# Gates, branch projections and merge by channel, merged in place; output product finished for one half of the tokens before the other

## What is computed

```python
up = jnp.einsum('bsnc,ncd->bsnd', branches, w_branch[l])
g = jax.nn.sigmoid(gate.reshape(B, S, N_BRANCH, D) + b_gate[l].reshape(N_BRANCH, D))
mixed = jnp.sum(g * up, axis=2) @ w_out[l]
h = layer_norm(DEEPNORM_ALPHA * h + mixed, ln1_g[l], ln1_b[l])
moe = hier_moe(h, ...)          # 16 experts, top-1 group of 4, top-2 within it
h = layer_norm(DEEPNORM_ALPHA * h + moe, ln2_g[l], ln2_b[l])
```

## Time and profile before

| what | before |
|---|---|
| median of three runs | 497.06 us |
| the profiled execution's own time | 497.06 us |
| its span in the profile | 495.3 us |
| PE busy | 458.8 us (93%) |
| DVE busy | 252.9 us (51%) |
| ACT busy | 158.8 us (32%) |
| POOL busy | 81.6 us (16%) |
| read from HBM | 139.46 MB |

### The profile page before, as it was taken

The page is one execution under the profiler, slowest core; times in us unless marked ns, Lnnn a source line. Parts: engine busy times, 40 slices in busy tenths (PEclk is TensorE's granted clock), DMA queues, the critical chain, the costliest instruction groups (busy, mean ns, idle before and its releaser), DMA issues.

```text
span 495.3 us, 6108 instructions
## 1 busy us (share of the span) xinstructions
PE 458.8 (93%) x2390; PEld 292.1 (59%) x2390; DVE 252.9 (51%) x493; ACT 158.8 (32%) x242; POOL 81.6 (16%) x76
## 2 busy tenths in 40 slices
PE   7999999999999999899679999999999999897880
PEld 7889998777777777778554334443353334432330
DVE  6079979978876857775571223222222221131237
ACT  3177373446553693610452001101040001000020
POOL 8865900000000004870700000000000000000000
PEclk9999999999999999999879999999999999999996
DMA  8990444444434369079956999999999999999922
GB/s 262 294 366 21 163 171 169 171 169 147 164 130 143 102 253 337 1 315 408 411 225 210 414 409 409 409 410 408 411 408 411 409 411 409 409 411 409 410 101 85
DMA packets 51417, 140.84 MB, mean 284 GB/s; under 512 B 6673, under 2 KB 10906, under 8 KB 51393
## 3 DMA queue, kind: packets, MB, share of 16 engines
q1 hardware_dynamic: 49856, 137.67, 73.1%
q10 hardware_dynamic: 1056, 2.65, 1.5%
q0 software_dynamic: 480, 0.20, 0.3%
HBM read 139.46 MB, written 1.05 MB: 284 GB/s over the span
## 4 chain that ended last, share of the span: by engine, by line
PE 59%; SPq 24%; DVE 7%; DMA 5%; ACT 3%; issue 2%; POOL 1%; DVEq 0%; ACTq 0%; POOLq 0%
SPq L450 24%; PE bank L1090 16%; PE bank L1349 9%; PE bank L996 6%; PE bank L1372 4%; PE bank L1236 4%; DMA ring<-in_expert_w_down_dram 4%; PE bank L967 4%; PE bank L1216 3%; PE bank L1287 2%; PE bank L1297 1%; PE bank L1009 1%; PE bank L1083 1%; PE bank L1021 1%; PE bank L945 1%
## 5 line engine op out<-in xcount | busy, mean ns | idle before, releaser
L1349 PE MATMUL bank<-ring,gates 128*64 128x512 f32 x512 | 115.0, 600 | 6.6 <-DMA ring<-in_expert_w_up_dram 4.4
L1090 PE MATMUL bank<-rounded 128*128 128x512 f32 x384 | 91.6, 394 | 0.0
L1090 PEld LDWEIGHTS bank<-rounded 128*128 128x128 f32 x384 | 70.8, 188 | 18.0 <-issue 4.0
L1349 PEld LDWEIGHTS bank<-ring,gates 128*64 128x64 f32 x512 | 35.8, 138 | 77.2 <-issue 65.9
L1372 PE MATMUL bank<-ring,gates 128*64 128x512 f32 x256 | 58.2, 598 | 1.2 <-DMA ring<-in_expert_w_down_dram 1.2
L1899 DVE SCALAR_TENSOR_TENSOR gates<-gates,bank 128x512 f32<-128x512 f32 x8 | 6.0, 748 | 81.5 <-PE bank L1349 81.5
L1513 DVE TENSOR_TENSOR rounded<-ring,rounded 128x1024 fp32r<-128x1024 f32 x32 | 37.0, 1222 | 13.3 <-ACT rounded L717 13.3
L1910 DVE TENSOR_TENSOR rounded<-bank,rounded 128x512 fp32r<-128x512 f32 x16 | 11.1, 692 | 53.5 <-ACT rounded L913 42.2
L1372 PEld LDWEIGHTS bank<-ring,gates 128*64 128x64 f32 x256 | 17.0, 136 | 35.3 <-issue 28.7
L717 ACT ACTIVATE rounded<-ring 128x1024 fp32r<-128x1024 f32 x32 | 31.2, 1053 | 4.5 <-PE bank L996 4.4
L996 PE MATMUL bank<-rounded 128*128 128x256 f32 x240 | 29.6, 284 | 0.0
(11 more groups left out here) (258 smaller groups left out, 562.5 us busy)
## 6 DMA issues: line engine op xcount, KB each, us to landing
ring<-in_expert_w_up_dram SPq DMA_DIRECT2D x32, 1024.0 KB, 18.2
ring<-in_expert_w_down_dram SPq DMA_DIRECT2D x32, 1024.0 KB, 18.4
ring<-in_expert_w_gate_dram SPq DMA_DIRECT2D x32, 1024.0 KB, 17.6
ring<-in_w_in_dram SPq DMA_DIRECT2D x10, 2048.0 KB, 7.9
ring<-in_w_branch_dram SPq DMA_DIRECT2D x2, 2048.0 KB, 7.9
ring<-in_w_out_dram SPq DMA_DIRECT2D x2, 2048.0 KB, 10.4
ring<-in_w_in_dram SPq DMA_DIRECT2D x3, 1024.0 KB, 13.7
ring<-in_w_in_dram SPq DMA_DIRECT2D x1, 1280.0 KB, 9.2
```

The source lines that it names most:

```text
L1090: last = pe.matmul(bank[:, b, :], hT_part[hpart][:, k, b * P:(b + 1) * P], w[wpart][:, k, :], start=False, stop=(k == KC - 1 and hpart == 1))
L1349: last = pe.matmul(bank[CAP * e:CAP * e + CAP, part // 2, :], xg[:, FC * h + k, c:c + CAP], w[:, e, k // 2, k % 2 * HALF:(k % 2 + 1) * HAL ...
```

## The change

Gates and branch projections are computed by channel instead of by token: the weights become the stationary operand and all 256 tokens are streamed. Each result is 128 channels x 256 tokens, so the gate bias is one number for each partition and goes into ACT's instruction (`bias=vcol[...]`); the bias matmuls and what built their operands go. The bias rows are fetched by POOL's queue as 32 rows and turned by one further transpose.

The merge goes chunk by chunk (`c`, 8 of them, 128 channels each): `up(c)` on PE for all four branches, then DVE multiplies into `gates` in place, adds two and two, then one and one, and writes the rest after ACT has rounded. The turned copy, its transposes and POOL's adds go. `out_part(c, t)` takes one chunk for one half of the tokens and both `j`; half 0 is completed first. `w_branch`'s second half gets its rounded part over `work` and `ln1p` (`rounded[11]`) instead of slot 5, so slot 5 can be loaded with expert weights before the merge. Which slots the first eight expert loads take, and after what, is new too (`EXPERT_SLOT`, `s_ohalf`).

```diff
-        WB_PART = [(1, SLOT["wb0"]), (5, SLOT["wb1"])]
+        WB_PART = [(1, SLOT["wb0"]), (RING + 3, SLOT["wb1"])]
+        def gated(c):
+            return gates[:, c // 4, :].rearrange("p (n c t) -> p n c t", n=NB, c=4)[:, :, c % 4, :]
+        def merged_part(c, part):
+            at = ((2 + part) * 4 + c % 4) * T
+            return rounded[RING + c // 4][:, at:at + T]
...
+        EXPERT_SLOT = (5, 6, 7, 2, 1, 3, 0, 4)
...
+            load_part(sp, 0)
+            sp.wait_ge(s_brlo, NB)
+            load_part(sp, 1)
+            load_part(sp, 2)
             sp.wait_ge(*USED["wb1"])
...
+            load_part(sp, 3)
+            sp.dma_start(ln1p[:, 0, :], a["ln1_g"][0].partition_broadcast(P)).then_inc(s_lnp, 16)
+            sp.dma_start(ln1p[:, 1, :], a["ln1_b"][0].partition_broadcast(P)).then_inc(s_lnp, 16)
+            sp.wait_ge(s_ohalf, 1)
+            for n in range(4, RING):
+                load_part(sp, n, (0,))
             sp.wait_ge(s_o, 4)
+            for n in range(4, RING):
+                load_part(sp, n, (1,))
...
-                        if pair == 0:
-                            pool.tensor_tensor(o, gated[0][:, 0], gated[0][:, 1], ALU.add).then_inc(s_mix, 2)
-                        else:
-                            link(pool.tensor_tensor(gated[1][:, 0], gated[1][:, 0], gated[1][:, 1], ALU.add))
-                            pool.tensor_tensor(o, o, gated[1][:, 0], ALU.add).then_inc(s_mix, 2)
...
+                for c in (2 * b, 2 * b + 1):
+                    r = NROW + n * KC + dq * 4 + c
+                    last = act.activation(gated(4 * dq + c)[:, n, :], bank[:, b, c % 2 * T:(c % 2 + 1) * T],
+                                          ACT.Sigmoid if dq else ACT.Identity, bias=vcol[:, r:r + 1])
...
             gate_out(7, 0)
+            loaded(act, "wb1")
...
+            for q in range(4):
+                c = slice(q * QUARTER, (q + 1) * QUARTER)
+                act.activation(rounded[WB_PART[1][0]][:, c], ring[:, SLOT["wb1"], c], ACT.Copy)\
+                    .then_inc(s_wbhi, 1)
             act.wait_ge(s_czT, 1)
...
+            for c in range(KC):
+                merged_rounded(c)
+                if 2 <= c < 6:
+                    act.wait_ge(*USED["wb0"])
+                    w_out_rounded(c - 2)
...
-                pe.matmul(bank[:, b, :], bias_pick[:, t:t + 1].broadcast_to([BIAS_ROWS, P]), bias_parts,
-                          start=True, stop=False)
...
+                            last = pe.matmul(bank[:, b, c * T:(c + 1) * T], w[wpart][:, k, at:at + P],
+                                             hT_part[hpart][:, k, :], start=(k == 0 and hpart == wpart),
+                                             stop=(k == KC - 1 and hpart == 1))
...
+            def up(c):
...
+                if c == 1:
+                    pe.wait_ge(s_gsig[1], 8)
+                if c >= 2:
+                    pe.wait_ge(s_mixp, c - 1)
+                for n in range(NB):
+                    if c % 4 == 0:
+                        pe.wait_ge(s_wblo[dq], n + 1)
+                        pe.wait_ge(s_brlo, NB if n == 3 else NB - 1)
+                    for kc in range(2):
+                        for wpart, bpart in PRODUCTS:
+                            last = pe.matmul(bank[:, at + n // 2, n % 2 * T:(n % 2 + 1) * T],
...
+            def out_part(c, t):
+                for j in range(2):
+                    w = [rounded_slot(i) for i in WO_PART[j]]
+                    pe.wait_ge(s_mTlo, c + 1)
+                    pe.wait_ge(s_wolo, c // 2 * 2 + j + 1)
...
+                if (c, t) == (3, 1):
+                    last.then_inc(s_ohalf, 1)
+            for c in range(6):
+                up(c)
+            out_part(0, 0)
+            up(6)
+            out_part(1, 0)
+            up(7)
+            for c in range(2, KC):
+                out_part(c, 0)
+            for c in range(KC):
+                out_part(c, 1)
...
+            for q in range(4):
+                branch_weights_rest(1, q)
             dve.wait_ge(s_cbr, 1)
...
+            for c in range(KC):
...
+                dve.tensor_tensor(g, bank[:, at:at + 2, :].rearrange("p a (n t) -> p (a n) t", n=2), g,
+                                  ALU.mult).then_inc(s_mixp, 1)
+                if c:
+                    merged_rest(c - 1)
+                dve.wait_ge(s_mixp, c + 1)
+                link(dve.tensor_tensor(g[:, 0:2], g[:, 0:2], g[:, 2:4], ALU.add))
+                dve.tensor_tensor(g[:, 0], g[:, 0], g[:, 1], ALU.add).then_inc(s_mix, 1)
+                if 4 <= c < 7:
+                    out_weights_rest((0, 1, 0)[c - 4], (0, 0, 1)[c - 4])
             out_weights_rest(1, 1)
+            merged_rest(KC - 1)
+            for q in (2, 3):
+                for j in range(2):
+                    out_weights_rest(j, q)
```

More of the change, by code:

```diff
@@ L444, in hybrid_trunk_kernel, with load_part @@
         PART_USED = (m_g0, m_g, m_u0, m_u, m_d0, m_y)
-        def load_part(eng, s, pair, part):
-            src = expert_part(pair, part)
-            for e in range(2):
+        def load_part(eng, n, halves=range(2)):
+            s = EXPERT_SLOT[n % RING]
+            src = expert_part(*divmod(n, 6))
+            for e in halves:
                 eng.dma_start(expert_slot(s)[:, e], src[:, e]).then_inc(s_slot[s], 8 * 2)
@@ L1190, in _ @@
             pe.wait_ge(s_poolo, 1)
-            def turn_merged(i):
-                pe.wait_ge(s_mix, 8 * (i // 2 + 1))
-                if i < 2:
-                    pe.wait_ge(s_lg, 4)
-                else:
-                    pe.wait_ge(s_mTlo, i - 1)
-                for kk in range(2):
-                    for t in range(TB):
-                        k = 2 * i + kk
-                        last = pe.transpose(bank[:, 4 + i % 2, kk * T + t * P:kk * T + (t + 1) * P],
-                                            work[:, t, k * P:(k + 1) * P], ident[:, :])
-                last.then_inc(s_mT, 1)
@@ L1206, in out_part @@
-            def out_part(j, t, k0, k1):
-                if k0 == 0:
-                    pe.wait_ge(s_mixp, 13 + 2 * t + j)
-                w = [rounded_slot(i) for i in WO_PART[j]]
-                for k in range(k0, k1):
-                    if k % 2 == 0:
-                        pe.wait_ge(s_mTlo, k // 2 + 1)
-                        pe.wait_ge(s_wolo, 4 * (k // 4) + 2 * j + k // 2 % 2 + 1)
-                    for mpart, wpart in ((0, 0), (0, 1), (1, 0)):
-                        last = pe.matmul(bank[:, 2 * t + j, :], merged_part[mpart][:, k, t * P:(t + 1) * P],
-                                         w[wpart][:, k, :], start=(k == 0 and mpart == wpart),
-                                         stop=(k == KC - 1 and mpart == 1))
-                if k1 == KC:
-                    last.then_inc(s_o, 1)
@@ new lines, in out_part @@
+            def out_part(c, t):
[3 more added lines that the diff above has]
+                    pe.wait_ge(s_wolo, c // 2 * 2 + j + 1)
+                    for mpart, wpart in PRODUCTS:
+                        last = pe.matmul(bank[:, 4 + 2 * t + j, :], merged_part(c, mpart)[:, t * P:(t + 1) * P],
+                                         w[wpart][:, c, :], start=(c == 0 and mpart == wpart),
+                                         stop=(c == KC - 1 and mpart == 1))
+                    if c == KC - 1:
+                        last.then_inc(s_o, 1)
+                if (c, t) == (3, 1):
+                    last.then_inc(s_ohalf, 1)
@@ L1355, in _ @@
                     pe.wait_ge(m_cTo, it + 1)
+                    pe.wait_ge(m_zero, 1)
                     pe.wait_ge(m_ylo, it * 2 + 1)
```

262 lines of the change are left out of this document (71 added, 191 removed).

## The result

The changed kernel takes 501.19 us, median of 8 runs from 499.69 to 502.45. The kernel before, run 8 times beside it, has a median of 495.95 over all eight; one of them, the disturbed one of 672.07 that also stands ahead of the prediction, is left out of the ratio. The ratio is 1.0100 with a 95% interval of 1.0083 to 1.0117: slower by 1.0%, which is clear of the noise of these runs and under the 2% from which on the prediction counts a change. The forecast was 501.0. The profiled execution took 501.31 us with a span of 499.5.

A forecast was written before the change was run, and what follows sets the result against it. PE alone was taken to bound the gates and nearly the products, DMA transfers the experts, whose length is fixed. -3.0 + 4.6 - 1.0 + 3.3 = +3.9 us on 497.06 gave 501.0 us, range 493 to 508.

The forecast's parts named there:

- The gates, -3.0: Gate tiles: 256-column matmuls without bias matmuls save 0.45 us a tile, bringing the end of tile 6 3.0 us earlier.
- T: End of gate tile 6's second half, where ACT takes it up: 171.5 us before, forecast 168.5.
- Into the branch product, 3.0 of wait: In `up(0)`, PE waits 3.0 us for the convolution branch, behind four more ACT instructions.
- The merge: Branch and output products: the order of DVE's `w_out` rests makes PE wait 1.0, 3.2 and 3.3 us.
- Waits and work together, +4.6: Last output matmul ends at T + 69.1 instead of T + 64.5: +4.6 us, bounds -6.5 to +7.
- Layer norm and router, -1.0: After the output product: half 1's transposes start 4.1 us after the last matmul, before 4.77; -1.0 us, bounds 0 and -2.5.
- The clock, +3.3: Behind the three new PE gaps: two of three drop the clock to half speed; +3.3 us, bounds 0 and 9.5.
- B and C: PE waits: B around `out_part(0, 0)`, forecast 1.0 and 3.2 us; C before j=1's half of `out_part(2, 0)`, forecast 3.3.
- A: PE's wait in `up(0)` before the fourth branch's products, forecast 3.0 us.
- The waits are hidden: Rival, from T on: DVE and ACT keep ahead, PE's 58.0 us is all; 486.6 us, chance 0.08.
- Half of them: Rival, merge waits: the order bites once only, or the clock stays up throughout; 494 to 498 us, chance 0.12.
- Three long drops: Rival: in each of three gaps the clock drops for 6.3 us, +9.5 for +3.3; 507.2 us, chance 0.10.

The follow-up runs named there:

- run 8: Not a label: the words say the kernel before was run 8 times beside the changed kernel, median 495.95 us.
- the silu's experiment: Changed kernel with ACT's silu ahead of the quarters of `w_branch`'s second half, last gates behind them, and DVE's rest of that branch ahead of those quarters' rests: 499.35 us.
- PE's order: Changed kernel with all eight chunks of the branch product ahead of the first output piece on PE, DVE's list untouched: 494.66 us.
- DVE's order: Changed kernel with DVE's j=1 rests of `w_out`'s first and second quarters moved up behind chunks 4 and 6, PE's list untouched: 496.72 us.
- PE's list in pairs: Changed kernel with all of `up` first, then output chunks 0 to 3 for both token halves in turn, then 4 to 7 per half: 490.97 us.
- the clock held in all three gaps: Changed kernel with spare transposes on PE: 24 in `up(0)` before the fourth branch, 22 and 24 before the output product's two long waits: 496.09 us.
- the late loads: Changed kernel with the first four expert loads moved behind the last chunk of the branch product: 500.85 us.
- the order in pairs with the silu moved: Changed kernel with all of `up` first, output pieces in pairs, and the silu and its rests ahead of `w_branch`'s second-half quarters: 487.83 us.
- 485.59 with the clock held: Changed kernel with output pairs and early silu, plus spare transposes in three waits behind the merge and 14 ahead of `up(1)`'s wait: 485.59 us.
- the first experiment: Changed kernel with 22 and 24 spare transposes on PE ahead of the output product's two long waits, before j=1 of pieces (0,0) and (2,0): 497.79 us.

## Why the prediction was right

**The gates, -3.0.** T came at 168.28 where ACT takes the tile up, forecast 168.5, before 171.57: -3.3. A tile took 11.78 us for the 11.71 counted.

**Into the branch product, 3.0 of wait.** Measured 3.25, and put down to DVE's rest of the convolution branch; the silu stood exactly behind the four quarters. The terms of ACT's list add up to 16.77 us and not to the 16.9 written, and ACT needed 16.4; the fourth branch began 17.7 us after T for the 18.0 counted. That `up(1)`'s gate would be nearly late behind it was right too: the silu's experiment found it as the next wait.

**The merge.** Forecast waits 1.0, 3.2 and 3.3; measured 1.06, 2.73 and 3.24. The middle one is shorter because from the end of one rest to the end of the other DVE takes 3.66 us where I laid 3.9 end to end, and PE's three matmuls ahead of it take 0.93 for my 0.68. The cause was named, and each end of it is shown by its own experiment: PE's order and DVE's order. The rival that DVE's pace sets the merge is out, since with PE's list in pairs the same DVE work hid completely.

**Waits and work together, +4.6.** With the clock held in all three gaps the last output matmul ended at 236.77 in the profile, T + 68.5 with T at 168.31, for T + 69.1 forecast.

**Layer norm and router, -1.0.** From the product's end to the first expert matmul 21.05 us (240.79 to 261.84), before 22.2 (236.0 to 258.2): -1.15. The second half's transposes began 4.15 us after the product's end (4.1 forecast) and took 1.19 us, not the 1.97 of the earlier trace rows: the clock was up there and fell later.

**The clock, +3.3.** The term that was undersized. Two of three gaps dropped it in the profiled run, as I counted, but one stretch was of the long kind, 6.8 us at 0.50. The other profiles say that two of three was luck of this execution: in each of the three with B and C unchanged (the changed kernel, the late loads, the early silu) both dropped it, at 1.3 to 2.4 us for B and 1.5 to 1.7 for C, and A dropped it in four of the six that have A without fillers, at 1.3 to 2.3 us. Against the rows of the kernel with the clock held, the stretch from 206.3 to the end of B's `up` cost 2.4 us and that behind C 1.7, together 4.1. Over the medians it is 501.19 - 496.09 = 5.1. The sum of the other terms was +0.6; by the runs it is 0.0 to 0.1. The total was met to 0.2 us because errors cancelled: the clock 1.8 too low, the other terms 0.6 too high, and the base 1.1 too high, since I set out from 497.06 where the median of before is 495.95. The increase itself was 5.2 us where I had 3.9. So the mechanism was right, and that the total was met so closely is luck.

**What costs nothing.** Shown for the expert loads. `ln1p` and POOL's clearing were not tried by themselves; POOL's additions with `ln1p` began at 241.97, 0.15 us after the transposes that released them, so `ln1p` was not late, and no wait of the profile up to 265 us is put down to POOL's clearing.

**The fixed length of the experts.** 237.7 us from their first matmul to the end, forecast 237, with the DMA at 0 GB/s just before. In the other kernels' profiles it was 235.8 to 238.0. In the six under 236 the first 16 matmuls took 3.65 us; but they did so too in two of 236.9 and 237.1, so the clock at the start is not all of it, and the rest stays open. "The same 237" is good to 1.2 us.

**The rivals.** "The waits are hidden" was forecast at 486.6 and did not come; the order in pairs with the silu moved came near to it, 487.83 with one wait of 1.98 us left, and 485.59 with the clock held, there also around the layer norm. "Half of them" (496) came about as "the clock stays up throughout": 496.09. "Three long drops" did not come: the highest of eight runs was 502.45. Loads that come earlier shorten nothing, by the experiment with late ones. The 256-column matmuls stayed at 123 ns.

The Trainium skill (TensorE: Matmul & The Clock Gate, HAM oscillation), by which each gap would count and the sum be 502.6, agrees with the clock's total over the runs better than my two of three: 5.1 us for 4.95. It does not agree run by run: in the profile of the changed kernel gap A left the clock at 1.00, and in that of the first experiment it did not.

## What to carry to other kernels

When a change turns two engines' work into a fine chain, lay both lists side by side and ask for each operand how many instructions of the other engine stand ahead of it; here the same instructions in another order were worth 10 us. A wait on TensorE cost its own length here and, in part of the executions, 1.3 to 2.4 us more behind it, by the fall of the clock; where it couldn't be removed, spare transposes into an unused bank bought back the second part. Before counting on a removed instruction, price the shape that replaces it: up to T the bias matmuls were worth 7.5 us and the shape that came with their removal took 4.2 of that back.

## What the runs showed of the hardware that was not expected

The clock's fall behind a gap is not a property of the gap alone. The same wait of 3.25 us (A) left it at 1.00 in two profiles, that of the changed kernel and that of the pairs, and was followed by 1.3 to 2.3 us of loss in four others with the same instructions up to there. A wait of 1.97 us was followed by 0.51 for 3 us in one profile and by no loss in two others (20.42 us for the 168 matmuls with pairs and early silu, 14.66 for 120), and C's wait by no loss where it was 2.73 us (81 matmuls in 18.63 us with all of `up` first, against 20.28).

I take this scatter for most of what spreads a kernel's runs. For it: the spread was 1.3 and 1.6 us in the two kernels with all gaps of the products filled and 1.9 to 4.2 us in the other versions of the changed kernel but one, and of the ten runs of the first experiment the five under 497.5 us had a mean granted clock of 0.979 to 0.984 and the five over 498 one of 0.974 to 0.977. Against it: 0.5 us in the one with pairs alone, which has gap A, and whose four runs agree in time at granted clocks of 0.975 to 0.982; why stays open.
